# Starting attention's scores inside the last key/value projection unit of a two-block transformer kernel

## What is computed

```
for l in range(2):                       # last = (l == 1)
    ... first feed-forward, norm ...
    p  = u @ w_in[l]                     # queries (16 heads of 64), keys and values
    kv_c = uc @ w_in[l][:, 1024:]        # context tokens (queries too in layer 0)
    q_g, k_g normed and roped; q_w, k_w roped
    y_w = window attention of heads 0..5 (2 kv heads, a sink column)
    y_g = global attention of heads 6..9 (2 kv heads)
    y_n = neighbourhood attention of heads 10..15 (a bias table)
    h  = h + gm * (concat(y_w, y_g, y_n) @ w_out[l])
    if not last:                         # the context attends to itself
        hc = hc + cgm * (context attention @ w_out[l])
    ... second feed-forward ...
```

## Time and profile before

| | |
|---|---|
| median of 3 runs | 2105.56 us (2104.94 to 2105.74) |
| the profiled execution, own time | 2104.8 us |
| its span in the profile | 2102.7 us |
| mean granted TensorE clock | 0.989 of full speed |
| TensorE busy | 2039.5 us, 97% of the span |
| attention of layer 0, last key/value unit to end of the loop | 836.87 to 943 us |
| attention of layer 1, the same | 1799.65 to 1877 us |

### The profile page before, as it was taken

The page is one execution under the profiler, slowest core; times in us unless marked ns, Lnnn a source line. Parts: engine busy times, 40 slices in busy tenths (PEclk is TensorE's granted clock), DMA queues, the critical chain, the costliest instruction groups (busy, mean ns, idle before and its releaser), DMA issues.

```text
span 2102.7 us, 28665 instructions
## 1 busy us (share of the span) xinstructions
PE 2039.5 (97%) x11483; PEld 1738.8 (83%) x11483; DVE 1418.7 (67%) x1989; ACT 800.2 (38%) x1136; POOL 218.9 (10%) x131
## 2 busy tenths in 40 slices
PE   7989999999999999999999999999999999899998
PEld 7877877888888887679888888988888888689998
DVE  6668998688867568765688867656664346665443
ACT  4344576422222232863322222322222232564443
POOL 0010000000001101332000001000000101243431
PEclk9999999999999999999999999999999999999999
DMA  5439797466545453102656555356564335115654
GB/s 174 132 84 297 266 309 223 131 180 172 173 135 166 126 165 100 41 2 80 180 165 184 166 146 165 97 150 189 176 179 126 97 119 150 61 41 148 185 165 144
DMA packets 415033, 314.89 MB, mean 150 GB/s; under 512 B 27551, under 2 KB 373542, under 8 KB 414902
## 3 DMA queue, kind: packets, MB, share of 16 engines
q1 hardware_dynamic: 375344, 237.43, 38.7%
q10 hardware_dynamic: 39558, 75.64, 11.7%
HBM read 311.97 MB, written 1.05 MB: 149 GB/s over the span
## 4 chain that ended last, share of the span: by engine, by line
PE 86%; DVE 7%; ACT 3%; issue 1%; DMA 1%; SPq 1%; ACTq 0%; DVEq 0%
PE ps L2125 24%; PE ps L2127 24%; PE ps L2126 24%; DVE w_lo L1231 3%; PE ps L2118 3%; PE ps L2929 2%; ACT w_hi L746 2%; PE ps L2896 1%; PE ps L2671 1%; PE ps L2673 1%; PE ps L2672 1%; SPq L708 1%; DVE u_lo L1324 1%; DVE tmp_a L1316 1%; PE ps L2704 1%
## 5 line engine op out<-in xcount | busy, mean ns | idle before, releaser
L2125 PE MATMUL ps<-u_hi,w_hi 128*128 128x512 f32 (+2 forms) x2112 | 740.5, 351 | 16.8 <-DVE u_lo L1324 7.0
L2126 PE MATMUL ps<-u_lo,w_hi 128*128 128x512 f32 (+2 forms) x2112 | 730.1, 346 | 0.0
L2127 PE MATMUL ps<-u_hi,w_lo 128*128 128x512 f32 (+2 forms) x2112 | 730.0, 346 | 0.0
L1231 DVE TENSOR_TENSOR w_lo<-raw,w_hi 128x2048 fp32r<-128x2048 f32 (+1 forms) x215 | 451.7, 2101 | 219.9 <-ACT w_hi L746 219.7
L746 ACT CAST w_hi<-raw 128x2048 fp32r<-128x2048 f32 (+1 forms) x215 | 374.9, 1745 | 449.3 <-PE ps L2127 409.9
L2125 PEld LDWEIGHTS ps<-u_hi,w_hi 128*128 128x128 f32 x2112 | 402.3, 190 | 69.0 <-DVE w_lo L1231 8.3
L2127 PEld LDWEIGHTS ps<-u_hi,w_lo 128*128 128x128 f32 x2112 | 402.2, 190 | 47.8
L2126 PEld LDWEIGHTS ps<-u_lo,w_hi 128*128 128x128 f32 x2112 | 402.5, 191 | 46.5
L1257 DVE SCALAR_TENSOR_TENSOR ada_acc<-ada_w,sc_c,ada_acc 128x512 f32<-128x512 f32 x448 | 318.5, 765 | 5.7
L2125 PE MATMUL ps<-hf_hi,w_hi 128*128 128x512 f32 (+1 forms) x770 | 268.5, 349 | 0.3
L2127 PE MATMUL ps<-hf_hi,w_lo 128*128 128x512 f32 (+1 forms) x770 | 266.8, 347 | 0.0
(11 more groups left out here) (404 smaller groups left out, 2141.6 us busy)
## 6 DMA issues: line engine op xcount, KB each, us to landing
ada_w<-in_w_ada ACTq DMA_DIRECT2D x144, 512.0 KB, 3.8
raw<-in_w_ffn_gate SPq DMA_DIRECT2D x88, 512.0 KB, 4.0
raw<-in_w_ffn_up SPq DMA_DIRECT2D x88, 512.0 KB, 5.3
raw<-in_w_in SPq DMA_DIRECT2D x52, 512.0 KB, 4.9
raw<-in_w_ffn_down SPq DMA_DIRECT2D x64, 384.0 KB, 3.3
raw<-in_w_ffn_down SPq DMA_DIRECT2D x64, 320.0 KB, 3.9
raw<-in_w_expert_down SPq DMA_DIRECT2D x26, 512.0 KB, 5.0
raw<-in_w_expert_gate SPq DMA_DIRECT2D x25, 512.0 KB, 5.1
```

Of the source, the lines that this page charges most:

```text
L1231: tt(low, full, high.bitcast(F32), ALU.subtract).then_inc(lo_done.sem, 1)
L2125: mm(acc, w1, m_hi, start=(first and i == 0), stop=False)
L2126: mm(acc, w1, m_lo, start=False, stop=False)
L2127: ins = mm(acc, w2, m_hi, start=False, stop=(last and i == n - 1))
```

## The change

Three parts of score work move in front of the end of the fifth key/value unit, in both layers:

- TensorE runs the fifth unit in four parts of 12 products. `scores(0)` follows part 0, `pre_work(4)` and `scores(1)` part 1, `scores(2)` part 2. Score unit 1 gets banks 6 and 7, so that it needs no bank of the fifth unit. After part 3 comes the loop from i = 3, whose first step is `turns(0)`, `scores(3)`, `pre_work(5)`; from i = 4 the order is as before.
- VectorE drops `split_lo` of the first output unit behind unit 3, and copies the fifth unit only after `logits(0)`, `logits(1)`, `sums(0)`, that `split_lo`, `logits(2)` and `sums(1)`. ScalarE loads the exponential's table ahead of the `k_sw` copies, and runs `exps(0)`, `pre_work(4)`, `halved(0)`, `exps(1)`, `halved(1)`, `exps(2)`, `pre_work(5)` before its loop.
- The second output unit is split at loop step i == N on both engines, that is, when the last scores have been given out.

The diff, cut to its core:

```diff
         def score_banks(l, i):
-            return 2 * ((layers[l]["out"]["g0"] + i) % 2)
+            return 6 if i == 1 else 2 * ((layers[l]["out"]["g0"] + i) % 2)
...
# ScalarE
-                linear(L["kv"], behind=pre_work, keep_last=1)
-                pre_work(5)
+                linear(L["kv"], behind=pre_work, keep_last=1, units=4)
...
-                for i in range(N + 5):
-                    if 3 <= i < N + 3:
+                exps(0)
+                pre_work(4)
+                halved(0)
+                exps(1)
+                halved(1)
+                exps(2)
+                pre_work(5)
+                for i in range(EARLY, N + 5):
+                    if i < N + 3:
                         outs(i - 3)
...
-                    if i == 1:
-                        u = L["out"]["u0"] + 1
-                        split_hi(u)
+                    if i == N:
+                        split_hi(L["out"]["u0"] + 1)
...
# VectorE
-                       tail=None if last else 15, behind=pre_work, keep_last=1)
+                linear(L["kv"], to_keys, tail=None if last else 15, behind=pre_work, keep_last=2, units=4)
...
+                logits(0)
+                logits(1)
+                sums(0)
+                split_lo(L["out"]["u0"])
+                logits(2)
+                sums(1)
+                kv = L["kv"]
+                dve.wait_ge(unit_done.sem, kv["u0"] + 5)
+                b = 2 * ((kv["g0"] + 4) % 2)
+                to_keys(4, ps[:, b:b + 2, :]).then_inc(acc_free.sem, 1)
+                for i in range(EARLY, N + 5):
...
-                    if i == 2:
-                        u = L["out"]["u0"] + 1
-                        split_lo(u)
...
+                    if i == N:
+                        split_lo(L["out"]["u0"] + 1)
...
# TensorE
+                        if n == PRE_ORDER.index(("value", VC + 1)):
+                            pe.wait_ge(A["exped"].sem, A["exped"].at(2))
...
-                    if i < 2:
-                        pe.wait_ge(acc_free.sem, acc_free.at(L["kv"]["g0"] + 4 + i))
+                    if i == 0:
+                        pe.wait_ge(acc_free.sem, acc_free.at(L["kv"]["g0"] + 4))
+                    if i == 1:
+                        pe.wait_ge(A["rot"].sem, A["rot"].at(7))
+                    if i == EARLY:
+                        pe.wait_ge(acc_free.sem, acc_free.at(L["kv"]["g0"] + 5))
...
-                scores(0)
-                pre_work(5)
-                scores(1)
-                scores(2)
-                pe.wait_ge(A["pre_act"].sem, A["pre_act"].at(8))
-                for i in range(3, N + 4):
-                    if i < N:
+                kv = L["kv"]
+                begin(kv["u0"] + 4, kv["g0"] + 4)
+                for part, (t, k0) in enumerate(((0, 0), (0, 4), (1, 0), (1, 4))):
+                    ins = products(ps[:, 2 * ((kv["g0"] + 4) % 2) + t, 0:T2], (kv["u0"] + 4) % 2,
+                                   [linear_cols(t, k) for k in range(k0, k0 + 4)], rows_of(u_hi, u_lo, k0, 4, T2), T2, k0 == 0,
+                                   k0 == 4)
+                    if part == 3:
+                        ins.then_inc(unit_done.sem, 1)
+                    if part == 1:
+                        pre_work(4)
+                    if part < EARLY:
+                        scores(part)
+                pe.wait_ge(A["pre_act"].sem, A["pre_act"].at(6))
+                for i in range(EARLY, N + 4):
+                    if i < N and i > EARLY:
                         scores(i)
...
                     if i < N + 3:
                         turns(i - 3)
+                    if i == EARLY:
+                        scores(i)
+                        pre_work(5)
+                    if i == EARLY + 1:
+                        pe.wait_ge(A["pre_act"].sem, A["pre_act"].at(8))
```

More of the change, by code:

```diff
@@ L441, in taken_with @@
             return 0 if tile < KA else (tile - KA) // 2 + 1
+        EARLY = 3
         def score_banks(l, i):
-            return 2 * ((layers[l]["out"]["g0"] + i) % 2)
+            return 6 if i == 1 else 2 * ((layers[l]["out"]["g0"] + i) % 2)
         OUT_BANKS = ((1, 3), (6, 7))
@@ L773, in square, with linear @@
                 nc.scalar.activation(tmp_b[:, slot, 0:T], row(h, k, first, first + T), ACT.Square).then_inc(n["sq"].sem, 1)
-            def linear(stg, squares=None, ada=None, behind=None, keep_last=0):
-                for i in range(stg["units"]):
+            def linear(stg, squares=None, ada=None, behind=None, keep_last=0, units=None):
+                for i in range(stg["units"] if units is None else units):
                     for c, quarter in ada_of_unit(ada, i)[0]:
@@ L1131, in pre_work @@
                         pre_square(KB)
+                    if i == 3:
+                        nc.scalar.activation(root_one[:, :], one, ACT.Exp)
                     if i in (2, 3):
@@ L1136, in pre_work @@
                         nc.scalar.copy(k_sw[HD:P, w, :], proj2[0:HD, t, :]).then_inc(A["k_sw"].sem, 1)
-                    if i == 3:
-                        nc.scalar.activation(root_one[:, :], one, ACT.Exp)
-                linear(L["kv"], behind=pre_work, keep_last=1)
-                pre_work(5)
+                linear(L["kv"], behind=pre_work, keep_last=1, units=4)
                 N = len(A["units"])
@@ L1182, in _ @@
                         exps(i)
-                    if 1 <= i < N + 1:
+                    if i < N + 1:
                         halved(i - 1)
-                    if i == 1:
-                        u = L["out"]["u0"] + 1
-                        split_hi(u)
+                    if i == N:
+                        split_hi(L["out"]["u0"] + 1)
                 linear(L["out"], (f"l{l}c", h2, TQ), keep_last=1)
@@ L1953, in pre_work, with to_keys @@
                             dve.wait_ge(A["roped"].sem, A["roped"].at(pre_count(("rope",), n + 1)))
-                linear(L["kv"], lambda i, acc: nc.vector.tensor_copy(proj2[:, 8 + 2 * i:10 + 2 * i, :], acc),
-                       tail=None if last else 15, behind=pre_work, keep_last=1)
+                def to_keys(i, acc):
+                    return nc.vector.tensor_copy(proj2[:, 8 + 2 * i:10 + 2 * i, :], acc)
+                linear(L["kv"], to_keys, tail=None if last else 15, behind=pre_work, keep_last=2, units=4)
                 N = len(A["units"])
@@ L2865, in _ @@
                 pe.wait_ge(nl.sem, nl.at(2 * KD))
-                linear(L["kv"], T2, tail=None if last else 15, behind=pre_work)
+                linear(L["kv"], T2, tail=None if last else 15, behind=pre_work, units=4)
                 N = len(A["units"])
```

## The result

The changed kernel takes 2094.58 us (median of 5 runs, 2093.71 to 2096.55), the kernel before 2105.74 on the same chip (5 runs, 2104.94 to 2106.55). The ratio is 0.9947, with a 95% interval of 0.9936 to 0.9958: faster, by 9 to 13 us. The forecast was 2092.9, its range 2090.5 to 2098. The profiled execution took 2095.22, its span is 2093.2.

What follows compares the result with a forecast made beforehand. TensorE, busy for 97% of the span, was taken to bound the kernel. Layer 0's 5.7 us and layer 1's 7.0 make 12.7, from 2104.8 to 2092.1; with 0.76 for the median, 2092.9 us, range 2090.5 to 2098.

Steps and rivals of the forecast that it cites:

- What bounds, and where the loss is: TensorE bounds the kernel; the loss is at the entry into attention, 7.7 us in layer 0 and 8.8 in layer 1.
- Layer 0's entry, 6.3 us: From the fifth unit to `scores(5)` in layer 0: `scores(5)` starts 6.3 us earlier than 865.58.
- the three switches: In the fifth unit, TensorE's three new returns from float32 work to split products cost 0.19 us each, 0.57 per layer.
- The sign given for them: In the fifth unit, three `L2125` products would be followed after 0.42 us.
- Layer 1's entry, 7.0 us: From the fifth unit to `scores(6)` in layer 1: `scores(6)` starts 7.0 us earlier.
- ScalarE's lead in the loop, 0.6 us: Layer 0's loop: ScalarE's lead melts by 0.25 us a unit; TensorE waits 0.6 us in the last three context units.
- Late splits cost nothing at the loop's end: At the loop's end the second output unit's moved splits cost nothing, at most 0.3 us; its weights have time to spare.
- GpSimd against VectorE: Behind `sums(0)`, VectorE's `split_lo` goes ahead of GpSimd's first scaling, which ends at 851.4, 0.9 us ahead of `turns(0)`.
- the other order: GpSimd's first scaling ahead of VectorE's `split_lo`: gain 1.8 us smaller in both layers together, 2094.7 us; chance 0.03.
- The sum, 12.7: Whole kernel: layer 0 gains 6.3 - 0.6 = 5.7 us and layer 1 7.0, together 12.7.
- The clock didn't fall, inside the unit or behind it: Rivals had it fall at the entry (2096.9 or 2100.9 us, chance 0.13) or inside the fifth unit (2119, chance 0.03).
- Rival 1: ScalarE and VectorE bound the loop, not TensorE: gains 4.8 and 5.5 us, together 10.3, so 2095.3; chance 0.15.

Runs made afterwards that it cites:

- split_at_entry: The changed kernel with the second output unit's splits moved back near the entry, at loop steps 3 and 4; ratio to the kernel before 0.9961.
- warm_before: The kernel before, with extra transposes that compute nothing used in TensorE's gaps at the entry of both layers; ratio to the kernel before 1.0001.
- half_copy: The changed kernel with VectorE copying the fifth unit in two pieces, the first tile after part 1; ratio to the kernel before 0.9934.
- three_on_gpsimd: The changed kernel with GpSimd scaling three of four probability blocks, instead of two, in layer 0's context units 2 to 7; ratio to the kernel before 0.9934.
- half_and_three: The changed kernel with the two-piece copy of the fifth unit and GpSimd's third block together; median 2093.96 us, ratio to the kernel before 0.9936.

## Why the prediction was right

By its own steps:

- **What bounds, and where the loss is.** Right: the time taken out at the entries stayed out, but for 1.10 us in layer 0's loop. The early scores alone hold the clock at 1.00 and give 8.2 us; the late splits bring that to 12.0.
- **Layer 0's entry, 6.3 us.** Measured 28.71 - 22.60 = 6.11. From the unit's first product to `turns(0)` are 855.37 - 839.93 = 15.44, worked out 15.4, so the three switches cost together about what was taken, 0.5 for 0.57. The sign given for them was not quite right: the first product behind scores is followed after 0.33 or 0.34 us (844.04 to 844.38), not 0.42, and in two of the three the last product ahead of the scores takes 0.32 instead of 0.23. The idle time ahead of `scores(3)` is 0.65 (taken 0.55), at `turns(1)` 0.24 (taken 0.25).
- **Layer 1's entry, 7.0 us.** Measured 32.89 - 25.86 = 7.03, with 0.44 for 0.55 and 0.25 for 0.25.
- **ScalarE's lead in the loop, 0.6 us.** The mechanism was right, the size was not: 1.10 us (L0 gains 5.01 of the entry's 6.11). This is the term that was mis-sized. Three steps up to `turns(6)` lose 0.27 or 0.28 each, 0.8 together, to ScalarE, in the three units that were named. Four more, from `turns(8)` to `turns(12)`, lose 0.07 to 0.09 each, though they are not context units. Their bound is not ScalarE but VectorE, which needs 3.18 us a step there, with the remainders of finished context pairs (`ylo`) still in it, against TensorE's 3.10; with the leads used up nothing covered it. I had let the loss end with the context units and counted ScalarE alone. The experiment that shortens ScalarE's step takes back all of the 1.10, VectorE's part too, by giving back the lead.
- **Late splits cost nothing at the loop's end.** Right: L1 is 7.02 shorter, as much as its entry. TensorE waits for no weights at the output units. The one wait for `w_lo` behind the loop, 0.65 us, is at 2069 in the FFN. Behind layer 1's loop the kernel before has none, but such waits of 0.2 to 1.1 us, at places that change, stand in all other traces, also in split_at_entry (1.04) and warm_before (0.21 and 0.24), which don't split late; so they don't need the late split. What brings them is open.
- **GpSimd against VectorE.** Right: VectorE is first, GpSimd ends 1.9 us late and nobody waits. The price of the other order was put at 1.8 and measured at 2.4: layer 1 was costed too low.
- **The sum, 12.7.** It is 12.03: 0.5 less by ScalarE's lead, 0.2 less by layer 0's entry. The rest of the 1.7 us between 2092.9 and 2094.58 is within what whole runs scatter by.
- **The rivals.** The clock didn't fall, inside the unit or behind it (1.00). Rival 1 holds in part: ScalarE bounds layer 0's loop for three steps and VectorE for four, not for all of it, and neither bounds layer 1's. Its layer 0 price, 4.8, was nearer to the measured 5.01 than the forecast's 5.7; in layer 1, 5.5 against a measured 7.02, it was wrong.

One thing the prediction didn't say: which half of the change gives what. Moving two splits, 1.8 and 2.3 us long, past the loop gives 5.9 us by itself, nearly half.

## What to carry to other kernels

At the entry of a pipelined loop, look not only at what TensorE waits for but at every long piece of other work that stands in the same queue ahead of the small ones it waits for; moving it past the loop costs a line. When TensorE gains at the entry, the engines that work beside it start the loop with a smaller lead. For each of them, multiply the difference of the steps by all units in which its step is longer than TensorE's, the ones that finish earlier units' work too: here ScalarE in the context units, then VectorE in the window units. And where whole runs scatter by more than the gain, compare stretches between two fixed instructions: here they repeat to 0.02 us in two traces of one kernel.

## What the runs showed of the hardware

**Much of the scatter of the traced executions comes from two stretches whose code no experiment touches, by their granted clock.** Windows of 50 us, some 690 us ahead of layer 0's fifth unit, of the kernel before, of the kernel after, and of its unchanged copy:

```profile
100.00:150.00 50.00, 43.78 (x308) 39.01 (x308) 35.02 (x60) 15.86 (x28) 7.24 (x6) 0.86 0.27 74
```

```profile
100.00:150.00 50.00, 43.67 (x291) 38.95 (x290) 34.12 (x56) 14.78 (x26) 7.21 (x6) 0.81 0.24 63
```

```profile
100.00:150.00 50.00, 43.78 (x311) 39.01 (x310) 35.24 (x62) 16.17 (x29) 7.23 (x6) 0.87 0.25 74
```

At 0.86 or 0.87 layer 0's fifth unit starts at 836.5 to 839.6 (eight traces), at 0.81 at 839.8 to 840.0 (three). The same program has both: the change started it at 839.93 in one execution and at 836.51 in another. That is the 3.06 us above, but for 0.4 us that stand already at 20 us. The clock of this window doesn't explain all starts: half_copy (839.56) and three_on_gpsimd (838.73) have 0.87 and 0.86, and are late by 2.7 and 2.1 us already at one of TensorE's first weight products, which starts at 20.70 us in the kernel before and at 23.40 and 22.80 in them. The second stretch lies ahead of layer 1's fifth unit, windows of before, after and warm_before:

```profile
1724.56:1799.65 75.09, 69.69 (x375) 60.37 (x374) 48.00 (x59) 22.96 (x27) 6.75 (x1) 0.98 0.50 143
```

```profile
1722.61:1796.59 73.98, 68.52 (x378) 59.20 (x377) 47.96 (x59) 23.27 (x27) 6.75 (x1) 1.00 0.51 145
```

```profile
1723.90:1801.45 77.55, 71.27 (x376) 61.53 (x374) 47.97 (x59) 22.97 (x27) 6.71 (x1) 0.96 0.49 139
```

The stretch takes 73.98 us at 1.00, 75.09 at 0.98 and 77.55 at 0.96; all eleven traces fall into these three groups, with 73.8 to 74.0, 75.0 to 75.7, and 76.75 (half_and_three) and 77.55. So the 2.5 us that warm_before has more here than the kernel before, in this one execution, take the place of the 2.0 that it gains at the entries. Since half_and_three has 0.96 there without extra work, it can be chance, but one execution can't tell. The timed runs (11 of warm_before, 15 of before) say only that the gain of 2 us doesn't reach the time.

**Engines that exclude each other.** A two-input VectorE instruction of 2.26 us and GpSimd's pair of scalings, begun 0.18 us after it, took 2.26 and 3.77 us; alone the pair takes 1.83. The Trainium skill, "SBUF — State Buffer", section "Who interferes with whom", has it that the second to issue waits for the whole of the first. 3.77 is 1.83 and 1.94 of waiting, so the trace agrees. The order decides the cost, as predicted: nothing with VectorE first, and 2.4 us instead of the expected 1.8 in the other order, which a semaphore forced.
